# The up product of each expert in tiles of 32 stationary columns instead of 64, in a mixture-of-experts trunk

## The reference

```python
def one_block(args):
    t, g, ex = args
    h = x_pad[t] @ w_gate_up[ex]                           # 1024 -> 512, the up product
    h = jax.nn.silu(h[:, :EXPERT_DIM]) * h[:, EXPERT_DIM:] # 256 wide
    return (h @ w_down[ex]) * g[:, None]                   # 256 -> 1024, the down product
...
out = jnp.zeros((n + 1, d), y.dtype).at[row_tok].add(y.reshape(rows, d))
```

## Time and profile before

| | |
|---|---|
| median of 3 runs (lowest, highest) | 1482.02 us (1481.56, 1483.02) |
| profiled execution: span from first to last instruction | 1479.2 us |
| its own time beyond the span | not recorded; the median of the runs is 2.8 us above the span |
| mean granted TensorE clock | 0.997 |
| PE, weight loads, DVE, ACT busy | 1462.7, 929.2, 568.5, 437.2 us |
| a pair step | 14.58 us (groups of six), 64 in all |
| its up product in the chain | 6.87 us |
| its down product in the chain | 3.58 us |

### The profile page before, as it was taken

How to read it: one execution, slowest core, us unless ns; L and a number is a source line. 1 busy time by engine, 2 the same in 40 slices (tenths; PEclk the granted TensorE clock), 3 DMA queues, 4 the chain that set the end, 5 groups by cost and what they waited for, 6 DMA issues and landing times.

```text
span 1479.2 us, 21063 instructions
## 1 busy us (share of the span) xinstructions
PE 1462.7 (99%) x8698; PEld 929.2 (63%) x8698; DVE 568.5 (38%) x970; ACT 437.2 (30%) x713; POOL 32.8 (2%) x30
## 2 busy tenths in 40 slices
PE   9999999999999999999999999999999999999996
PEld 8999999544444444444399999984444444444442
DVE  4567856222212222221555777661222212222124
ACT  4565543211111212111336544432111121211112
POOL 0111000000000000000001100000000000000000
PEclk9999999999999999999999999999999999999998
DMA  8654459899999999999835544688999999998993
GB/s 310 209 200 159 152 202 385 335 426 424 427 424 427 424 425 424 415 420 424 344 114 181 175 148 171 259 339 370 424 426 423 428 423 427 424 426 363 421 423 136
DMA packets 80586, 497.67 MB, mean 336 GB/s; under 512 B 6320, under 2 KB 11696, under 8 KB 47472
## 3 DMA queue, kind: packets, MB, share of 16 engines
q1 hardware_dynamic: 78208, 492.69, 82.2%
q10 hardware_dynamic: 2288, 3.67, 0.7%
HBM read 493.99 MB, written 1.05 MB: 335 GB/s over the span
## 4 chain that ended last, share of the span: by engine, by line
PE 95%; DVE 2%; DMA 1%; ACT 1%; issue 0%; SPq 0%; DVEq 0%
PE bank L1696 30%; PE bank L1529 19%; PE bank L1723 16%; PE bank L1649 8%; PE bank L1676 8%; PE bank L1594 5%; PE bank L1484 3%; PE bank L1710 1%; PE bank L1422 1%; DMA ring_w<-in_w_in 1%; PE bank L1541 1%; PE bank L1667 1%; PE bank L1658 1%; PE bank L1567 1%; PE bank L1550 1%
## 5 line engine op out<-in xcount | busy, mean ns | idle before, releaser
L926 DVE TENSOR_TENSOR w_lo<-ring_w,w_hi 128x2048 fp32r<-128x2048 f32 x71 | 162.4, 2289 | 102.0 <-ACT w_hi L701 101.9
L1529 PE MATMUL bank<-x_hi,w_hi 128*128 128x256 f32 x704 | 201.0, 286 | 0.3 <-DVE w_lo L926 0.3
L1529 PE MATMUL bank<-x_lo,w_hi 128*128 128x256 f32 x704 | 199.2, 283 | 0.0
L1529 PE MATMUL bank<-x_hi,w_lo 128*128 128x256 f32 x704 | 199.2, 283 | 0.0
L1340 DVE TENSOR_TENSOR y_lo<-bank,y_hi 128x512 fp32r<-128x512 f32 x128 | 88.5, 691 | 199.0 <-ACT y_hi L843 199.0
L1325 DVE SCALAR_TENSOR_TENSOR hid<-hid,gate_s,bank 128x256 f32<-128x256 f32 x64 | 30.8, 481 | 348.9 <-ACT hid L827 348.9
L701 ACT CAST w_hi<-ring_w 128x2048 fp32r<-128x2048 f32 x71 | 135.1, 1904 | 50.7 <-PE bank L1594 30.5
L843 ACT CAST y_hi<-bank 128x512 fp32r<-128x512 f32 x128 | 75.0, 586 | 252.0 <-PE bank L1723 252.0
L827 ACT ACTIVATE hid<-bank 128x256 f32<-128x256 f32 x64 | 24.5, 384 | 404.1 <-PE bank L1696 404.1
L1529 PEld LDWEIGHTS bank<-x_hi,w_hi 128*128 128x128 f32 x704 | 135.0, 192 | 2.4 <-issue 0.7
L1529 PEld LDWEIGHTS bank<-x_lo,w_hi 128*128 128x128 f32 x704 | 135.1, 192 | 0.1
(11 more groups left out here) (231 smaller groups left out, 2017.6 us busy)
## 6 DMA issues: line engine op xcount, KB each, us to landing
arena<-in_expert_w_gate_up SPq DMA_DIRECT2D x24, 4096.0 KB, 17.2
gu_a<-in_expert_w_gate_up SPq DMA_DIRECT2D x24, 4096.0 KB, 17.0
ring_w<-in_expert_w_gate_up SPq DMA_DIRECT2D x32, 2048.0 KB, 15.8
ring_w<-in_w_in SPq DMA_DIRECT2D x25, 2048.0 KB, 8.6
arena<-in_expert_w_down SPq DMA_DIRECT2D x24, 2048.0 KB, 14.9
dn_a<-in_expert_w_down SPq DMA_DIRECT2D x24, 2048.0 KB, 14.8
dn_c<-in_expert_w_down SPq DMA_DIRECT2D x16, 2048.0 KB, 15.1
ring_w<-in_w_out SPq DMA_DIRECT2D x4, 2048.0 KB, 7.8
```

Of the source, the lines that this page charges most:

```text
L926: v.tensor_tensor(chunk_part(w_lo, n), chunk_in(n), chunk_part(w_hi, n).bitcast(F32), ALU.subtract).then_inc(w_lo_ready, 1)
L1529: ins = mm(b[:, S * c:S * c + S], lhs, rhs, start=(k == 0 and a + w == 0), stop=(k == KD - 1 and a == 1))
```

## The change

Each product of 56 stationary columns becomes two, one of 32 and one of 24 columns. They read the same moving slice and write partitions 0 to 31 and 32 to 55 for expert 0, and 64 to 95 and 96 to 119 for expert 1. A slice has four products where it had two. Nothing else is changed: the down product, the gathers, the waits and the semaphores stay.

```diff
-                        for e in range(2):
-                            c = USED * (2 * step + e)
-                            ins = mm(bank_up[SLOTS * e:SLOTS * e + USED, :], xe_t[g.half][:, k, c:c + USED],
-                                     gu[slot][:, e, k, :], start=(k == 0), stop=(k == KD - 1))
+                        for q in range(P // 32):
+                            at_slot, some = 32 * (q % 2), (32, USED - 32)[q % 2]
+                            c = USED * (2 * step + q // 2) + at_slot
+                            ins = mm(bank_up[32 * q:32 * q + some, :], xe_t[g.half][:, k, c:c + some],
+                                     gu[slot][:, q // 2, k, :], start=(k == 0), stop=(k == KD - 1))
                     ins.then_inc(up_done, 1)
```

## The result

The changed kernel takes 1490.8 us (median of 3 runs, 1489.92 to 1491.77) where the kernel before takes 1482.02: a ratio of 1.0058, 95% interval 1.004 to 1.0076. Timed again in five rounds beside the kernel before on one chip it took 1490.06 against 1481.21, a ratio of 1.0061 (1.0047 to 1.0074). It is slower by 0.6%, 8.8 us.

A forecast was written before the change was run, and what follows sets the result against it. PE was taken to bound the kernel. Width passage 7.5, stagger 1.0 and first steps -0.04 summed to 8.4 us, which on 1482.0 gave 1490.4 us; the 8-in-10 range was 1482.5 to 1502.

The forecast's parts named there:

- PE alone sets the pace of the expert stage: Expert stage: PE is busy throughout, so each nanosecond added to a pair step reaches the end, 64 times over.
- Streaming costs nothing, four at once: Up product: four 32-column tiles run at once, each round still 0.43 us, 6.87 us in all, change 0.
- rival B: Up product: not four tiles at once; two together add 440 us, three together 147 us; chance 0.12.
- The passage, 62 times 0.12 us: Between down (64-column tiles) and up (now 32): a paid width change, 0.095 fixed plus 0.026 load, 7.5 us in all.
- rival A: Between down and up: going from 64 to 32 columns is free, leaving only +1.0 us, 1483.0; chance 0.17.
- The upper bound: Down to up: 0.30 us each, 18.6 us in all, if the tiles' first loads don't overlap.
- The stagger, 15 ns x 64 = 1.0 us: End of each up product: the last of four tiles starts three small steps late instead of one; bounds 0 and 1.3.
- Issue and instruction fetch: Up product: 8 instructions per 0.43 us round leave issue room, change 0; fetch for 4096 more instructions is negligible.
- Waits: Expert stage: no wait is added, and the up product's wait for y_lo gets easier.
- The first steps, -0.04 us: First up product of each layer: exposed load of 26 ns in place of 45, two times.
- The signs: New profile: 592 ns records, up still 6.9 us, first record 26 ns longer, 0.52 us before up's load, steps of 14.72.

The follow-up runs named there:

- the mirror image: Against the kernel before the change: up product left in two tiles of 64, down product cut into four tiles of 32; 1489.62 us, ratio 1.0055.

## Why the prediction was right

*PE alone sets the pace of the expert stage.* Right: what a step loses arrives at the end, 8.53 us in the two expert stages of 8.9 in the span.

*Streaming costs nothing, four at once (against rival B).* Right: 592 ns a record and 0.43 us a round, and with the passage taken away the product takes 6.87 us with four tiles as it did with two.

*The passage, 62 times 0.12 us (against rival A).* Right, and it is the cause, shown by taking it away (1.0007), by moving it (1.006) and by multiplying it (0.137 to 0.139 us each). Its parts are as priced: 0.10 us longer from the last down start until the first up record (0.53 instead of 0.43), and 25 ns of load, together 0.125. 62 x 0.125 = 7.8 us for the 7.5 predicted. The upper bound, first loads one after the other, did not come: eight loads stand within 0.15 us.

*The stagger, 15 ns x 64 = 1.0 us.* The sum was about right: what the changed kernel has beside the passage is 8.5 - 7.8 = 0.8 us, and the run with two tiles at once gets back 0.88. The mechanism accounts for about half of it. The first record behind the up product starts 6.998 us after the up product's first one, against 6.991 with two narrow tiles and 6.967 before (medians of the 62 steps). So at the end of the up product, where the prediction puts the stagger, the two further tiles cost 7 ns, not 15: 0.4 us. The other 7 ns a step lie later in the step, and no run shows why. That the total comes so close is partly luck.

The longer gathers (1.44 us, before 1.42) are no measure of it. With two tiles at once in the up product they take 1.44 too, and with four and no passage 1.42: first the mirror image, then both products narrow.

```profile
453.93 1.44 PE bank L1649 x8
```

```profile
452.36 1.42 PE bank L1649 x8
```

So they are longer in steps with a passage, whatever the number of tiles; why is open.

*Issue and instruction fetch.* Right: no idle time of PE in the stage, and fetch moved 1.41 MB in 86 packets over the whole span, 1.15 MB in 70 before.

*Waits.* Right that none is added: over the same twelve steps, 284 to 462, the weight loads wait for "issue" and for hid_t alone, hid_t for 4.4 us as in the earlier trace rows.

*The first steps, -0.04 us.* Too small to be told in the runs; the trace has the shorter load there (617 against 637 ns).

*The signs.* The gap of 0.53 us, the 25 ns and the step of 14.73 us (0.52, 26 ns and 14.72 were named) came. One was named wrongly: the up product in the chain went to 7.00 us and did not stay at 6.9, because the passage stands at its front.

The Trainium skill's rule on the mode change, TensorEngine Tiling (Array Packing), Key Properties, holds between 64 and 32 in both directions, 0.125 and 0.14 us each. The Trainium skill's figure for three column tiles, 2.38 (TensorE: Matmul & The Clock Gate, Measured speedup vs the span model), could not be checked with three tiles, which no run has; with four, in an accumulation of 16 rounds, no such shortfall shows: a round of four records takes 0.43 us, as a single full-width one does.

## What to carry to other kernels

Count the changes of tile width on TensorE along its order of issue, not the number or the size of its products. In this kernel each one cost about 0.13 us between tiles of 64 and of 32, in either direction, between two products and inside one, and 0.21 from 64 into the full array; work of two widths did not run side by side. If one product is cut into narrower tiles, cut its neighbours alike, and the price is gone; but where tiles of 64 already run two at once, as here, nothing was gained by it. In a stage in which one engine is busy without a break, a sum over one step from the chain and from the gaps between single records can give the end time to about a microsecond: 8.4 us here for 8.8 measured.

## What was not expected

With both products narrow the whole program did not get faster, though the exposed loads are 25 ns shorter in each of 64 steps. The trace shows that this did pay in the expert stages: cut as above, they take 448.43 and 448.29 us, 0.21 and 0.41 less than before. The load in front of down is 25 ns shorter, and the four tiles give 13 of them back behind the up product (its first record to the next product's first: 6.980 us, before 6.967). That is a net gain of 12 ns a step, 0.7 us over 62 steps, close to the 0.62 of the two stages and to the 1.6 - 0.8 that I had expected.

The gain is lost elsewhere: the mixer of layer 2 takes 1.1 us longer. At the end of layer 1, TensorE's products wait for y_lo, which they do not in the kernel before:

```profile
PE bank L1767 <- DVE y_lo L1340: 1.0, 1, 1.0
```

VectorE is still making the mixer's w_lo there (line 926, from 731.55 us, 2.29 us long) and comes to y_lo only at 733.76, where it came to it at 732.31 before. Only one execution of this kernel has a trace, so it is not shown that the wait comes every time, nor whether the edit causes it.

And a product of 56 columns does not overlap with one of 32 in the other half of the array: mixing the two widths slice by slice adds 38% to the whole kernel's time.
